# Splitting the gate weights of the embedding one piece a step

## The reference, cut to what matters

```python
x = x + conv_ffn(rms_norm(x, ffn_norm_g[i]), w_gate[i], w_up[i], conv_w[i], conv_b[i], w_down[i])
gate = jax.nn.sigmoid(rms_norm(x, ple_norm_g[i]) @ w_ple_gate[i])
x = x + gate * (p[i] @ w_ple_proj[i])
```

## Time and profile before

| | |
|---|---|
| median of the runs | 2726.79 us |
| lowest and highest run | 2722.6, 2728.81 us |
| profiled execution | 2724.11 us |
| its span, first to last instruction | 2722.4 us |
| mean granted TensorE clock | 0.971 |
| PE busy | 94% of the span |
| DVE, ACT busy | 54%, 37% |

### The profile page before, as it was taken

How to read it: one execution, slowest core, us unless ns; L and a number is a source line. 1 busy time by engine, 2 the same in 40 slices (tenths; PEclk the granted TensorE clock), 3 DMA queues, 4 the chain that set the end, 5 groups by cost and what they waited for, 6 DMA issues and landing times. The chain is left out here.

```text
span 2722.4 us, 37132 instructions
## 1 busy us (share of the span) xinstructions
PE 2556.3 (94%) x14438; PEld 2194.8 (81%) x14438; DVE 1456.6 (54%) x2148; ACT 998.8 (37%) x1721; POOL 355.5 (13%) x450
## 2 busy tenths in 40 slices
PE   8969999999599998999997898999899999999989
PEld 6849999999488886888896786878788888888777
DVE  6523444442366763535225867645887877534342
ACT  4223222221255653223114776743433333223231
POOL 1002222220233230001002322101000000000000
PEclk9979999999699998999998998999999999999999
DMA  4222122111442224343224111154222222364422
GB/s 147 83 82 82 53 63 66 53 42 34 115 124 86 82 74 164 119 167 109 89 101 150 55 39 52 49 176 148 56 89 93 77 79 87 108 204 163 161 86 82
DMA packets 215846, 264.76 MB, mean 97 GB/s; under 512 B 46932, under 2 KB 147924, under 8 KB 215672
## 3 DMA queue, kind: packets, MB, share of 16 engines
q1 hardware_dynamic: 215672, 262.38, 30.4%
HBM read 185.11 MB, written 77.22 MB: 96 GB/s over the span
## 5 line engine op out<-in xcount | busy, mean ns | idle before, releaser
L1379 PE MATMUL delta_acc<-delta_w_hi,xn_hi 128*128 128x256 f32 x640 | 191.5, 299 | 2.9 <-DVE delta_w_lo L1333 2.9
L1381 PE MATMUL delta_acc<-delta_w_hi,xn_lo 128*128 128x256 f32 x640 | 181.0, 283 | 0.0
L1380 PE MATMUL delta_acc<-delta_w_lo,xn_hi 128*128 128x256 f32 x640 | 180.8, 282 | 0.0
L4500 DVE TENSOR_TENSOR ffn_feed_lo<-ffn_feed_raw,ffn_feed_hi 128x1536 fp32r<-128x1536 f32 x44 | 77.2, 1759 | 140.2 <-ACT ffn_feed_hi L4491 139.9
L4200 PE MATMUL ffn_up_acc<-mixed_hi,ffn_ring_hi 128*128 128x512 f32 x348 | 135.6, 390 | 1.8 <-DVE ffn_gain_row L4120 1.3
L4200 PE MATMUL ffn_up_acc<-mixed_lo,ffn_ring_hi 128*128 128x512 f32 x348 | 135.4, 389 | 0.0
L4200 PE MATMUL ffn_up_acc<-mixed_hi,ffn_ring_lo 128*128 128x512 f32 x348 | 135.4, 389 | 0.0
L426 DVE TENSOR_TENSOR_SCAN stick_keep<-stick_keep,stick_zero 128x127 f32<-128x127 f32 (+7 forms) x64 | 92.4, 1444 | 74.2 <-ACT stick_keep L378 73.4
L1379 PEld LDWEIGHTS delta_acc<-delta_w_hi,xn_hi 128*128 128x128 f32 x640 | 121.9, 190 | 8.9 <-issue 5.5
L4491 ACT ACTIVATE ffn_feed_hi<-ffn_feed_raw 128x1536 fp32r<-128x1536 f32 x44 | 65.2, 1485 | 162.8 <-PE ffn_up_acc L4570 157.1
L1380 PEld LDWEIGHTS delta_acc<-delta_w_lo,xn_hi 128*128 128x128 f32 x640 | 122.0, 191 | 0.0
(11 more groups left out here) (494 smaller groups left out, 7120.7 us busy)
## 6 DMA issues: line engine op xcount, KB each, us to landing
ffn_feed_raw<-in_w_down SPq DMA_DIRECT2D x44, 512.0 KB, 4.2
ffn_ring_raw<-in_w_gate SPq DMA_DIRECT2D x11, 1024.0 KB, 5.4
ffn_ring_raw<-in_w_up SPq DMA_DIRECT2D x11, 1024.0 KB, 5.4
scratch_act_t<-ffn_silu SPq DMA_DIRECT2D x22, 512.0 KB, 3.2
ffn_feed_raw<-scratch_act_t SPq DMA_DIRECT2D x44, 256.0 KB, 3.0
delta_w_raw<-in_w_in SPq DMA_DIRECT2D x20, 512.0 KB, 3.9
scratch_projected<-delta_out SPq DMA_DIRECT2D x80, 128.0 KB, 1.7
stick_g_raw<-in_w_in SPq DMA_DIRECT2D x16, 512.0 KB, 4.4
```

What stands on the lines that cost most here:

```text
L1379: nc.tensor.matmul(acc, self.hi[:, k, tok], w_hi, start=(k == 0), stop=False, skip_group_check=True)
L1380: nc.tensor.matmul(acc, self.hi[:, k, tok], w_lo, start=False, stop=False, skip_group_check=True)
L1381: last = nc.tensor.matmul(acc, self.lo[:, k, tok], w_hi, start=False, stop=(k == self.kt - 1), skip_group_check=True)
L4500: self.nc.vector.tensor_tensor(self.lo[s][:], self.raw[s][:], self.hi[s][:].bitcast(F32), ALU.subtract).then_inc(self.lo_done[s], 1)
```

## The change

A step of `GateWeights` loads at most one piece and splits at most one piece. Its ACT and DVE generators have an empty first step, and one more empty step ahead of piece 4. The plan has ten steps of `gates` in place of five: in rounds 2, 5, 7, 9 and 11, one behind the last round, and two behind each of the scalings of tiles 3 and 5. Step by step: round 2 loads piece 0; rounds 5, 7, 9 and 11 load pieces 1 to 4 and split 0 to 3; the step behind the loop loads piece 5; the two behind the scaling of tile 3 load pieces 6 and 7 and split 4 and 5; the two behind the scaling of tile 5 split 6 and 7. Buffers, sizes and waits of a load or a split are as before.

```diff
     def sync(self, sp):
-        self.load(sp, 0)
-        yield
         for i in range(8):
-            if i + 1 < 8:
-                self.load(sp, i + 1)
-            if i % 2:
+            self.load(sp, i)
+            yield
...
     def scalar(self, act):
         yield
         for i in range(8):
+            if i == 4:
+                yield
             act.wait_ge(self.loaded[self.buffer(i)], 16 * (len(self.before(i)) + 1))
...
             self.nc.scalar.activation(self.part(i, 0), self.raw[self.buffer(i)][:], ACT.Copy).then_inc(self.hi_done, 1)
-            if i % 2:
-                yield
+            yield

     def vector(self, dve):
         yield
         for i in range(8):
+            if i == 4:
+                yield
             dve.wait_ge(self.hi_done, i + 1)
...
-            if i % 2:
-                yield
+            yield
...
-        plan += [gates] * (i in (2, 8, 12))
-    plan += [down, down, down, turn, down, turn, scale, square, square]
-    plan += [square, square, ple, turn, gates, scale]
+        plan += [gates] * (i in (2, 5, 7, 9, 11))
+    plan += [gates, down, down, down, turn, down, turn, scale, square, square]
+    plan += [square, square, ple, turn, scale, gates, gates]
     plan += [ple, turn, scale]
-    plan += [ple, turn, gates, scale]
+    plan += [ple, turn, scale, gates, gates]
     plan += [ple, turn, scale]
```

## The result

The changed kernel takes 2705.14 us (median of 4 runs, 2701.07 to 2708.22), the kernel before 2726.53 us (4 runs). The ratio is 0.9923, with a 95% interval of 0.9908 to 0.9938. The profiled execution of the changed kernel took 2701.07 us, with a span of 2699.3 us.

The account below looks back on a forecast made before the run. PE was taken as the bound, busy 2556.3 of 2722.4 us. Removing 7.8 us in the down projection and 13.3 in the last stage took the median 2726.8 to 2705.7, stated as 2705.5; range 2700.5 to 2712.5.

Parts of the forecast that it names:

- The price of the four stalls: Two PE stalls in the down projection, two in the last stage: 21.12 us lost against PE's pace, 14.29 of it idle.
- the likeliest case: All four PE stalls, in down projection and last stage, gone: 2705.5 us, own range 2702 to 2709, chance 0.74.
- Part one: Down projection: one piece a step, loaded two rounds before its split, removes both PE stalls, 7.8 us.
- Part two: Around the loop's end: piece 4 loaded in round 11, piece 5 behind the loop; takes out a 3.10 us load wait.
- Part three: Last stage: the next tile's scaling on DVE goes ahead of the gate splits; 13.3 us taken for the last stage's stalls.
- The walk of DVE: Last stage: start times worked out operation by operation on DVE, with 0.2, 0.5 and 0.3 us as tightest spares.
- A: Rival: DVE becomes the bound of the last stage; misses of 0.3 us plus slow clock, 2711.5 us; chance 0.14.
- B: Rival: gate loads in the down projection push w_down chunk loads late; slower, 2734 us; chance 0.05.
- C: Rival: the last stage's stalls stay because piece 6 or 7 lands late; 2719 us; chance 0.07 together with D.
- D: Rival: pieces split in the loop are still waited for; 2713.5 at best, 2726 at worst; chance 0.07 with C.
- The slow clock: After PE stalls: refill and matmuls partly at 1.2 instead of 2.4 GHz, 6.83 us beyond idle time, varying between runs.
- the 6.83 us: Loss beyond idle PE at the four stalls, from refill and slow clock; counted in full though perhaps one draw.

Follow-up runs that it names:

- loop only: Changed kernel with the last stage as before (two pieces split ahead of each scaling, pieces 5 to 7 loaded there): 2718.79 us, stretch 206.11 us.
- last stage only: Changed kernel with the down projection's loop as before (two pieces a step in rounds 8 and 12): 2716.78 us, stretch 200.71 us.
- Load in the same step: Changed kernel, but in rounds 5, 7, 9 and 11 each piece is loaded and split in one step: 2715.22 us, stretch 203.80 us.
- after, again: The changed kernel unaltered, measured and profiled a second time: 2702.48 us, ratio 0.9919 to the kernel before, stretch 192.55 us.
- order alone: Changed kernel, scalings still ahead of the splits, but pieces 5 to 7 loaded in the last stage as before: 2704.69 us, stretch 194.88 us.
- one round apart: Changed kernel, but the loop's gate steps stand in rounds 2, 8, 9, 10 and 11: 2703.81 us, stretch 192.56 us.

## Why the prediction was right

**The price of the four stalls.** 21.12 us forecast from PE's pace, 21.10 measured. The prediction had this step right: lateness against an undisturbed round, and not idle time (14.3 us), is what comes back. The closeness to 0.02 us says only that no lateness is left, as the price was read from the same execution of the kernel before. By parts: 7.78 for the loop, 7.55 in "loop only", where the clock behind the two stalls that are left was slower; 13.34 for the last stage, 12.95 in "last stage only", where the two stalls that are left were longer.

**The forecast time.** 2705.5 us; measured 2705.14, and 2702.48 in the second set of runs, both in the likeliest case's own range. To hit the median within 0.4 us was luck: runs of one kernel spread by 3 to 10 us from causes ahead of the change.

**Part one.** ACT, DVE and SP had the room that I gave them: no `ffn_feed_hi` moved. The loads of pieces 0 to 4 landed within the 5.2 us that I allowed, so the 2.1 us to spare stood. "Load in the same step" shows which term carries it, the early load.

**Part two.** Piece 5's load went out at 2585.61, ahead of the loads of `ffn_emb_in`, and nothing waited for these.

**Part three.** The walk of DVE held to 0.1 us: moved by 2619.38 - 2609.62 = 9.76 us, my starts for `ffn_xn` 3 and 4 and for piece 6 are 2610.76, 2616.79 and 2623.13, and the trace has 2610.75, 2616.68 and 2623.22. Two sizes were off, without effect. For piece 7 I left out the 0.15 us from release to matmul that I had counted for `ffn_xn`, so its 0.3 us to spare was 0.15. And the slowest landing allowed for pieces 6 and 7, 5.2 us, was too short: piece 7's took 5.7 us, and one of the two took 6.1 in "after, again". ACT still had no wait.

**The rivals.** A (DVE the bound) didn't happen, though it was nearer than I wrote: 0.15 us. B (chunk loads pushed late) didn't in the changed kernel: they landed within 5.1 us (line 4466), below the 6.2 of the earlier trace rows. But its mechanism is real: "last stage only" has one chunk that ACT waits for behind a gate load. C and D didn't: ACT has no wait for a gate load left.

**The slow clock.** What a stall costs beyond its idle time differs from stall to stall, and not by its length alone: 0.3 us after 2.64 and 2.50, but 1.9 after 2.89 and 3.44, and the round behind one of 1.90 took 1.6 too long. In one kernel idle times of 2.77 and 2.17 brought the clock to about 0.8 and one of 1.55 between them didn't. That it is a draw from run to run isn't shown. The Trainium skill, "TensorE: Matmul & The Clock Gate", section "What's actually happening", counts slow matmuls at the start of a kernel and finds their number to differ between runs; the prediction carried this over to pauses. Here four stalls came again in a second kernel that keeps them, and cost nearly the same: 0.33 and 1.92 us beyond the idle time in the loop before, 0.32 and 1.89 in "last stage only"; next rounds 1.55 and 2.71 us too long in the last stage before, 1.66 and 2.85 in "loop only". No kernel with a stall was traced twice. With every stall gone the cost is gone too: 192.56 and 192.55 us in the two executions of the changed kernel. So the 6.83 us were worth their full size here.

What the prediction lacked: that the order and the early load overlap. It priced the last stage as one sum and would not have said that "order alone" gives 11.2 of 13.55 us.

## What to carry to other kernels

Where every engine runs one written list, a load that is awaited in the step that issues it holds up all that stands behind it on that engine. Issue it a step ahead, and put what the bounding engine wants next ahead of work that is due later. To price such a change, take the pace of the bounding engine from an undisturbed round and count how late each later round is; that includes the slow clock, and the idle time alone (14.3 of 21.1 us here) doesn't. To verify one of under one per cent, compare a stretch of the trace that begins where the programs begin to differ.

## What the runs showed that I had not expected

The same instructions ahead of the change take a different time in each execution, by up to 10 us, though the changed stretch repeats to 0.01 us. In "after, again" the matmuls of line 593 start for the last time at 1054.5 us and in "order alone" at 1055.3. These are the first and last starts of the matmuls of a later line in the two, and then the stretches between:

```profile
L4200 PE MATMUL ffn_up_acc<-mixed_hi,ffn_ring_hi x348: 387/389/477, 1939.5 to 2354.7; 128*128 128x512 f32 x174
```

```profile
L4200 PE MATMUL ffn_up_acc<-mixed_hi,ffn_ring_hi x348: 389/389/481, 1950.0 to 2365.1; 128*128 128x512 f32 x174
```

```profile
1054.50:1939.50 885.00, 820.52 (x4407) 689.99 (x4406) 475.37 (x989) 377.53 (x777) 121.05 (x227) 0.96 0.34 111
```

```profile
1055.30:1950.00 894.70, 826.24 (x4409) 693.24 (x4407) 475.63 (x989) 377.76 (x777) 121.15 (x227) 0.95 0.34 110
```

The two are 0.8 us apart at the end of the first line and 10.5 at the start of the second, and stay so to the end of it. Of the 9.7 us between, 5.7 is longer busy time of PE over the same matmuls, at a granted clock of 0.95 against 0.96, and 4.0 is more idle time (68.5 against 64.5 us). These two ran on different chips, but "one round apart", on the chip of "after, again", has the same shape: 891.9 us between the two lines, 826.1 of them busy. So more than half of the spread is slower matmuls. Which of the many short waits there sets it off stays open.
